# State products in a bank of their own, loads spread over chain steps, and a Horner form in the recurrent stage of a hybrid block

## The chip, the cores and the metric

The kernel runs on one core of a Trainium2 chip. The metric is the device time of the whole kernel in microseconds (us), the median of a few executions. TensorE is called PE below, its weight loads PEld, VectorE DVE, ScalarE ACT, GpSimd POOL, and SyncE SP. SP issues most of the DMAs.

## What is computed

The reference is one layer of a hybrid model on 1040 tokens (16 meta tokens and 1024 inputs) of width 1024: a norm, one input projection, an RWKV-7 recurrence over 16 heads of 64 dimensions, differential attention over 8 heads, a gated merge, and a mixture of 32 experts. The change touches the recurrence only:

```python
def step(state, inp):
    r_t, w_t, k_t, v_t, kk_t, a_t = inp
    sa = jnp.einsum('bhvk,bhk->bhv', state, -kk_t)
    state = (state * w_t[:, :, None, :]
             + sa[..., None] * (kk_t * a_t)[:, :, None, :]
             + v_t[..., None] * k_t[:, :, None, :])
    return state, jnp.einsum('bhvk,bhk->bhv', state, r_t)
```

## The kernel before

The kernel is a row of stages with a barrier between them: norm, two projections, attention, the recurrence (`rwkv`), merge, output and routing, experts, combine. The change lies in `rwkv`.

**Chunks.** The 1040 tokens are cut into 20 chunks of 52. Four heads are worked on at a time (index `d`, 0 to 3; `e` and `h` number the four heads, `h` being the upper or lower half of the partitions), so there are 80 chunks `ch`. A chunk has four kinds of work:

- `m` (`masked`): PE multiplies four pairs of chunk matrices for each head into PSUM (L1360), DVE masks the result into the tile `rw_M` (L1620). The PSUM bank is `ch % 2`, so bank 0 and bank 1 alternate.
- `tok`: PE turns three inputs by a product with the identity (L1435), ACT copies them to `rw_tok` (L1520).
- `solve`: a triangular inverse in steps 2, 6, 7, 8, 9, 10, 11, 12. Each step is a set of 52x52 products on PE and a copy by ACT (L1514) or an addition by DVE (L1634, L1644, L1631, L1649). Steps 10 to 12 make the second factor: step 10 gives Y and its transpose (copied by ACT to `rw_Y`), step 11 gives Y squared (copied by ACT), DVE makes G = I + Y from the copy in SBUF (L1631), and step 12 gives G + Y²G.
- `seq`: the chain over chunks, in steps q = 1 to 5. Step 1 multiplies the state by the keys (L1452, L1455), ACT negates it into `rw_R` (L1528). Steps 2 and 3 apply the two factors (L1459, L1464), each followed by an ACT copy (L1531, L1534). Step 4 makes the update of the state (L1471, L1473) in columns 384 to 511 of bank 6. DVE adds the old state (L1660, into `rw_St`) and multiplies by the chunk's decay `c.Pend` (L1662, into `rw_S`). Step 5 makes the chunk's output (L1479, L1481, L1484) in columns 256 to 383 of the same bank 6, and ACT copies it (L1541).

Before step 5 PE waits until DVE has finished with the bank:

```python
if t < NCH - 1:
    pe.wait_ge(seq_add, added(ch))
```

**Order.** `round_` writes the order out by hand. A round solves two chunks A and B at once, runs the chain for the two chunks of the round before, and makes the masked matrices of the two chunks ahead. There are 40 rounds and one more in which only the chain runs. Each engine walks the same list:

```python
return (step(2) + tokens(A) + piece() + step(6) + piece() + tokens(B) + step(7) + piece() + step(8) + piece() + piece()
        + step(9) + ahead(A + 2, 0) + piece() + step(10) + ahead(A + 2, 1) + piece() + step(11) + ahead(B + 2, 0) + piece()
        + step(12) + ahead(B + 2, 1) + piece() + piece())
```

The ten pieces of a round are q = 1 to 5 of one chunk and then of the next. A group norm over finished chunks (`gn`, seven times) is strewn over the pieces: DVE sums, ACT roots and evictions (L1549, L1559), POOL on large tiles (L1588 to L1603), PE transposes (L1497).

**Loads.** SP loads the five inputs of the next four heads in `load(d)`, ten DMAs of 520 KB back to back, once the chain has left the buffers. `load_rest(gi)` loads two more inputs for a group norm in four DMAs. `load_branch` brings in weights of the next stage. At the stage's start SP issues `load(1)`, two `load_branch`, `load_rest(0)` and `load_rest(1)`.

Of the kernel before, what the change touches and what calls it, by code (L numbers as in the profile page):

```python
# [12 lines left out]
ALU = mybir.AluOpType  # L13
# [7 lines left out]
TC = 52  # L21
NCH = T // TC
# [1186 lines left out]
def rwkv(nc, c):  # L1209

    with ExitStack() as st:
# [24 lines left out]
        Y1 = sb("rw_Y1", [128, 2, 2, 2, TC])  # L1236
        Y2 = sb("rw_Y2", [128, 2, 2, TC])
# [5 lines left out]
        St = sb("rw_St", [128, 2, RD])  # L1243
        bank = ps("rw_bank", [128, 8, 512])
        made, early_in = sem("rw_made"), sem("rw_early_in")
        emptied, tok_emptied = sem("rw_emptied"), sem("rw_tok_emptied")
# [3 lines left out]
        seq_dve, seq_act, seq_pe, seq_add = sem("rw_seq_dve"), sem("rw_seq_act"), sem("rw_seq_pe"), sem("rw_seq_add")  # L1250
# [7 lines left out]
        STEPS = {"pe": (2, 6, 7, 8, 9, 10, 11, 12), "dve": (2, 7, 8, 9, 11, 12),  # L1258
                 "act": (6, 7, 8, 10, 11), "pool": (6,)}
# [54 lines left out]
        @block.sync  # L1314
        def _(sp):
            def load(d):
                z = d % 2
                if d >= 2:
                    sp.wait_ge(seq_pe, seq_done(NCH * (d - 1) - 1, 5))
                for e in range(2):  # L1320
                    for dst, j in ((BK[z][:, e, 0], BHAT), (KR[z][:, e, 0], KAP), (KR[z][:, e, 1], RHAT), (BK[z][:, e, 1], KHAT),
                                   (V[z][:, e], VAL)):
                        sp.dma_start(dst, c.rwD[2 * d + e, j]).then_inc(x_in[z], 16)
# [24 lines left out]
        def _(pe):  # L1348
            def masked(ch, e):
                d, z, cols = place(ch)  # L1350
                if e == 0:
                    if ch == 0:
                        pe.wait_ge(emptied, 1 + OPEN)
                    if ch % NCH == 0:
                        pe.wait_ge(x_in[z], 160 * ((d + 1) // 2) + OPEN)
                    if ch > 1:
                        pe.wait_ge(m_read, ch - 1 + OPEN)
                for j in range(2):
                    for h in range(2):
                        last = mm(bank[here(h), ch % 2, (4 * e + 2 * j) * TC:(4 * e + 2 * j + 2) * TC].rearrange("p (a t) -> p a t", a=2),  # L1360
                                  BK[z][half(h), e, j, cols], KR[z][half(h), e, :, cols], start=True, stop=True)
                if e == 1:
                    last.then_inc(m_done, 1)

            def solve(ch, n):
# [4 lines left out]
                if n == 2:  # L1370
                    if ch == 0:
                        pe.wait_ge(emptied, 2 + OPEN)
# [66 lines left out]
            def seq(ch, q):  # L1439
# [25 lines left out]
                elif q == 4:  # L1465
# [3 lines left out]
                    for e in range(2):  # L1469
                        for h in range(2):  # L1470
                            mm(bank[half(h), 6, 384 + RD * e:384 + RD * e + RD], tok[here(h), s, 0, e, :], Uu[here(h), e, :], start=True, stop=False)  # L1471
                        for h in range(2):
                            last = mm(bank[half(h), 6, 384 + RD * e:384 + RD * e + RD], tok[here(h), s, 1, e, :], vv(e, h), start=False, stop=True)  # L1473
                else:
                    if t < NCH - 1:
                        pe.wait_ge(seq_add, added(ch))
# [27 lines left out]
        def _(act):  # L1504
            def solve(ch, n):
# [5 lines left out]
                        10: (Y1[0:PX, ln], four), 11: (Y2[0:PX, ln], two)}  # L1511
# [10 lines left out]
            def seq(ch, q):  # L1522
# [40 lines left out]
            nc.scalar.mul(bank[:, 6:8, :], c.eps[:].unsqueeze(2).to_broadcast([128, 2, 512]), 0.0).then_inc(tok_emptied, 1)  # L1563
# [4 lines left out]
        def _(pool):  # L1568
            over_heads = lambda j, n: gs[0:PX, j, 0:n].unsqueeze(2).to_broadcast([PX, n, RD])

            def solve(ch, n):
                ln = ch % 2
                eye = maskn[0:PX, 2].unsqueeze(1).to_broadcast([PX, 2, TC])
                if n == 6:
# [32 lines left out]
            walk({"solve": solve, "gn": norm})  # L1607

        @block.vector
        def _(dve):  # L1610
            tt, ts = nc.vector.tensor_tensor, nc.vector.tensor_scalar

            def masked(ch, e):
# [6 lines left out]
                tt(M4[0:PX, m], bank[0:PX, ch % 2, 0:8 * TC].rearrange("p (e k t) -> p e k t", e=2, k=4),  # L1620
                   mask4[0:PX].unsqueeze(1).to_broadcast([PX, 2, 4, TC]), ALU.mult).then_inc(m_read, 1)

            def solve(ch, n):
# [3 lines left out]
                if n in STEPS["dve"] and n != 11:  # L1627
                    dve.wait_ge(*at_pe(ch, n))
                if n == 11:
                    dve.wait_ge(*at_act(ch, 10))  # L1630
                    tt(G[0:PX, ln], Y1[0:PX, ln, 0], maskn[0:PX, 2].unsqueeze(1).to_broadcast([PX, 2, TC]),  # L1631
                       ALU.add).then_inc(sdve[ln], 1)
# [12 lines left out]
                elif n == 12:  # L1645
                    dve.wait_ge(*at_dve(ch, 11))
                    if ch >= TS4:
                        dve.wait_ge(seq_pe, seq_done(ch - TS4, 3))
                    tt(Gf[0:PX, ch % TS4], pairs(bq), G[0:PX, ln], ALU.add).then_inc(sdve[ln], 1)  # L1649

            def seq(ch, q):
                d, t = divmod(ch, NCH)
                if q == 4 and t < NCH - 1:
                    src = bank[:, 6, 384:512].rearrange("p (e d) -> p e d", e=2)
                    dve.wait_ge(seq_pe, seq_done(ch, 4))
                    if t == 0:
                        nc.vector.tensor_copy(St[:], src).then_inc(seq_add, 1)
                    else:
                        dve.wait_ge(seq_dve, added(ch - 1))
                        tt(St[:], src, S[:, t % 2], ALU.add).then_inc(seq_add, 1)  # L1660
                    dve.wait_ge(seq_add, added(ch))
                    tt(S[:, (t + 1) % 2], St[:], c.Pend[:, 2 * d:2 * d + 2, t:t + 1].to_broadcast([128, 2, RD]), ALU.mult).then_inc(seq_dve, 1)  # L1662
# [22 lines left out]
            nc.vector.memset(bank[:, 0:2, :], 0.0).then_inc(emptied, 1)  # L1685
            nc.vector.memset(bank[:, 2:6, :], 0.0).then_inc(emptied, 1)
# [1251 lines left out]
```

## Time and profile before

| | |
|---|---|
| time, median of 3 | 2832.94 us (2831.69 to 2835.86) |
| time of the profiled execution | 2827.87 us |
| its span, first to last instruction | 2826.1 us |
| the recurrent stage in it | from about 1212 us to about 1809 us of the span |
| mean granted TensorE clock, whole span | 0.966 |

The span is what the profile covers, and the device time of the same execution is 1.8 us longer. The stage begins where PE issues L1360 for the first time, and ends with the last copy of L1541 (it starts at 1807.82 us).

### The profile page before, as it was taken

The page shows a single profiled execution, that of the slowest core. Times are in us where ns is not written, and L with a number is a line of the kernel's source. Part 1 is how long each engine was busy: PE and PEld are TensorE (multiplying, and loading weights), DVE is VectorE, ACT ScalarE, POOL GpSimd, SP SyncE. Part 2 cuts the span into 40 slices and gives each one's busy share as a digit, 9 for nine tenths or more (in the row PEclk, how much of TensorE's full clock was granted, in tenths as well). Part 3 has the DMA queues.
Part 4 walks back from the last instruction along what each step waited for, and adds up shares of the span by engine and source line. Part 5 has one row for each costly group of instructions (what it writes and reads, how often), then busy time and mean ns, then how long its engine had stood idle before and what let it go on. Part 6 is the DMA issues. An engine that isn't in the chain of part 4 may idle for free. (4 is left out here: it accounts for less than half of the span.)

```text
span 2826.1 us, 64905 instructions
## 1 busy us (share of the span) xinstructions
PE 2584.2 (91%) x27593; PEld 2153.8 (76%) x27593; DVE 1571.1 (56%) x2294; ACT 1313.0 (46%) x2199; POOL 321.0 (11%) x367
## 2 busy tenths in 40 slices
PE   6999999999989999979888999799895999999992
PEld 5989886777766666778888888678784788888882
DVE  4566664442045555534344444553325888888885
ACT  5555542222134444324444444552222777777771
POOL 0121222331000000001212121200000000000002
PEclk9999999999999999989999999899996999999996
DMA  4443432212123224140202000144255999999976
GB/s 108 159 170 122 144 147 81 94 61 79 40 96 93 64 85 157 36 129 5 96 18 96 18 21 18 39 134 127 85 216 195 370 395 396 391 399 394 396 309 254
DMA packets 160693, 440.46 MB, mean 156 GB/s; under 512 B 14343, under 2 KB 94873, under 8 KB 148145
## 3 DMA queue, kind: packets, MB, share of 16 engines
q1 hardware_dynamic: 144461, 381.94, 37.6%
q10 hardware_dynamic: 9060, 29.56, 2.8%
q0 software_dynamic: 6912, 25.17, 2.3%
q8 instruction: 203, 3.33, 0.5%
q14 instruction: 57, 0.47, 0.1%
HBM read 344.22 MB, written 92.41 MB: 154 GB/s over the span
## 5 line engine op out<-in xcount | busy, mean ns | idle before, releaser
L2591 DVE TENSOR_TENSOR ex_wL<-wx,ex_wH 128x2048 fp32r<-128x2048 f32 x192 | 436.1, 2286 | 46.3 <-ACT ex_wH L2495 44.5
L2495 ACT CAST ex_wH<-wx 128x2048 fp32r<-128x2048 f32 x192 | 366.4, 1912 | 93.8 <-PE ex_bank L2391 70.6
L2389 PE MATMUL ex_bank<-ex_wH,ex_xTH 128*128 128x512 f32 x512 | 200.0, 391 | 2.4 <-DVE ex_xTL L2596 2.4
L2391 PE MATMUL ex_bank<-ex_wL,ex_xTH 128*128 128x512 f32 x512 | 199.8, 390 | 0.0
L2390 PE MATMUL ex_bank<-ex_wH,ex_xTL 128*128 128x512 f32 x512 | 199.7, 390 | 0.0
L709 PE MATMUL ph_acc<-ph_wH,uH 128*104 128x512 f32 x480 | 192.5, 401 | 6.5 <-DVE ph_wL L721 6.5
L709 PE MATMUL ph_acc<-ph_wH,uL 128*104 128x512 f32 x480 | 189.5, 395 | 0.0
L709 PE MATMUL ph_acc<-ph_wL,uH 128*104 128x512 f32 x480 | 189.5, 395 | 0.0
L413 PE MATMUL pf_acc<-uH,pf_wH 128*128 128x348 f32 x648 | 160.5, 356 | 6.3 <-DVE pf_wL L533 6.3
L413 PE MATMUL pf_acc<-uL,pf_wH 128*128 128x348 f32 x648 | 138.6, 322 | 0.0
L413 PE MATMUL pf_acc<-uH,pf_wL 128*128 128x348 f32 x648 | 138.3, 322 | 0.0
L413 PEld LDWEIGHTS pf_acc<-uH,pf_wH 128*128 128x128 f32 x648 | 110.7, 189 | 33.0 <-issue 11.6
L1644 DVE TENSOR_TENSOR rw_Q<-rw_bank,rw_Q 116x104 f32<-116x104 f32 x160 | 42.7, 267 | 158.8 <-PE rw_bank L1394 128.6
L1093 DVE TENSOR_REDUCE at_nmx<-at_bank 128x1 f32<-128x272 f32 (+7 forms) x128 | 93.0, 769 | 66.9 <-PE at_bank L1018 66.2
L1050 PEld LDWEIGHTS at_bank<-at_v,at_aT 128*128 128x128 f32 (+1 forms) x704 | 92.8, 189 | 45.9 <-ACT at_aT L1163 22.9
L2389 PE MATMUL ex_bank<-ex_wH,ex_hTH 128*128 128x512 f32 x256 | 103.9, 406 | 22.3 <-DVE ex_hTL L2601 22.3
L1050 PE MATMUL at_bank<-at_v,at_aT 128*128 128x128 f32 (+1 forms) x704 | 117.9, 296 | 4.1 <-ACT at_aT L1163 2.7
L1578 POOL TENSOR_TENSOR rw_Q<-rw_M,maskn 116x104 f32<-116x104 f32 x80 | 36.6, 459 | 745.1 <-DVE rw_M L1620 745.1
L1163 ACT COPY at_aT<-at_bank 128x512 f32<-128x512 f32 (+3 forms) x72 | 37.1, 515 | 175.3 <-PE at_bank L1040 175.3
L2389 PEld LDWEIGHTS ex_bank<-ex_wH,ex_xTH 128*128 128x128 f32 x512 | 96.5, 188 | 22.9 <-DVE ex_xTL L2596 2.8
L2391 PEld LDWEIGHTS ex_bank<-ex_wL,ex_xTH 128*128 128x128 f32 x512 | 96.4, 188 | 20.1
L2390 PEld LDWEIGHTS ex_bank<-ex_wH,ex_xTL 128*128 128x128 f32 x512 | 96.5, 188 | 20.0
(397 smaller groups left out, 6623.7 us busy)
## 6 DMA issues: line engine op xcount, KB each, us to landing
wx<-in_expert_w_gate SPq DMA_DIRECT2D x32, 2048.0 KB
wx<-in_expert_w_up SPq DMA_DIRECT2D x32, 2048.0 KB
wx<-in_expert_w_down SPq DMA_DIRECT2D x32, 2048.0 KB
s_y<-ex_y ACTq DMA_DIRECT2D x32, 512.0 KB, 10.1
fw<-in_w_in SPq DMA_DIRECT2D x27, 512.0 KB
hw<-in_w_in SPq DMA_DIRECT2D x6, 2048.0 KB, 10.1
s_qkT<-ph_stg ACTq DMA_DIRECT2D x4, 2080.0 KB, 6.9
mb_gt<-s_pT SPq DMA_DIRECT2D x16, 512.0 KB, 3.5
```

The source lines that it names most:

```text
L413: last = mm(acc[:, s, x, 0:CP], ww[:, s, k, :], uu[:, k, x * CP:(x + 1) * CP], start=(k == 0 and j == 0), stop=(k == KD - 1 and j == 2))
L709: last = nc.tensor.matmul(acc[:, slot, :], uu[:, k, t * TT:(t + 1) * TT], ww[:, b, k, :], start=(k == 0 and j == 0), stop=(k == KD - 1 and ...
L1050: last = nc.tensor.matmul(bank[:, PV:PV + 128], aT[0:rows_of(j), g % 2, 128 * x:128 * x + 128], v[0:rows_of(j), u // NS % 2, j, :], start= ...
L1093: nc.vector.tensor_reduce(nmx[:, u % 2, n:n + 1], bank[:, at:at + keys(u)], AX.X, ALU.max, negate=True).then_inc(maxed, 1)
L1163: nc.scalar.copy(aT[:, 0, 0:n], bank[:, TURN:TURN + n]).then_inc(moved_act, 1)
L1578: nc.gpsimd.tensor_tensor(Q[0:PX, ln, 0], M4[0:PX, ch % MS, :, 0, :], eye, ALU.add).then_inc(spool[ln], 1)
L1644: tt(dst, pairs(bq), Q[0:PX, ln, 1 - n % 2], ALU.add).then_inc(sdve[ln], 1)
L2389: nc.tensor.matmul(out, aH, bH, start=first, stop=False)
L2390: nc.tensor.matmul(out, aL, bH, start=False, stop=False)
L2391: return nc.tensor.matmul(out, aH, bL, start=False, stop=last)
L2495: nc.scalar.copy(wH[:, w, part], raw(j, s)[:, part]).then_inc(w_high, 1)
L2591: nc.vector.tensor_tensor(wL[:, w, part], raw(j, s)[:, part], wH[:, w, part], ALU.subtract).then_inc(w_low, 1)
```

## The change

Five things are changed in `rwkv`:

1. The state products of q = 4 go to bank 1, the masked matrices always to bank 0. PE no longer waits between q = 4 and q = 5; before each `m` it waits until DVE has read the chunk before.
2. The state update is split: ACT multiplies the old state by the decay after q = 1 (`SP`), and DVE does product times decay plus `SP` in one instruction for each `e`, in place of an addition and a multiplication.
3. The second factor is made by Horner's rule, I + Y(I + Y(I + Y)): PE makes the same number of products, ACT copies one 104-column tile at step 10 in place of a 208-column one and copies nothing at step 11, DVE adds the identity out of PSUM at steps 10, 11 and 12.
4. `load(d, n)` issues one DMA for each finished chain step (all five of its pieces), for ten chunks in a row. `load_rest(0)` comes first, the branch weights last. `load(1, 0)` waits for nothing.
5. The zeroing of PSUM at the start is shared out otherwise: DVE 416 and 1024 columns, ACT 624 in four pieces. POOL's copy of the diagonal block for step 7 moves forward in its own order, to the place of `m`.

```diff
             def load_rest(gi): ...
-            load(1)
+            load_rest(0)
+            for gi in range(1, 2 * ND):
+                if gi % 2 == 1 and gi // 2 + 1 < ND:
+                    for n in range(10):
+                        load(gi // 2 + 1, n)
+                load_rest(gi)
             for i in range(2):
                 load_branch(sp, c, c.w_branch_rwkv, c.bw[:, i], i, early_in)
-            load_rest(0)
-            load_rest(1)
-            for gi in range(2, 2 * ND):
-                if gi % 2 == 0 and gi // 2 + 1 < ND:
-                    load(gi // 2 + 1)
-                load_rest(gi)
+            def load(d, n):
+                z = d % 2
+                e, k = divmod(n, 5)
+                dst, j = (...)[k]
+                if d > 1 or n > 0:
+                    sp.wait_ge(seq_pe, seq_done(NCH * (d - 1) - 1 + n, 5))
+                sp.dma_start(dst, c.rwD[2 * d + e, j]).then_inc(x_in[z], 16)
 # PE, masked
-                    if ch > 1:
-                        pe.wait_ge(m_read, ch - 1 + OPEN)
+                    if ch > 0:
+                        pe.wait_ge(m_read, ch + OPEN)
-                        last = mm(bank[here(h), ch % 2, ...
+                        last = mm(bank[here(h), 0, ...
 # PE, solve
                 elif n == 10:
-                            mm(at(bx, 0, e, h), Nn[here(h), ln, 1, e, :], Qf[here(h), f, e, :], start=True, stop=True)
+                            mm(at(bx, 0, e, h), Qf[here(h), f, e, :], Nn[here(h), ln, 1, e, :], start=True, stop=True)
-                            last = mm(at(bx, 1, e, h), Qf[here(h), f, e, :], Nn[here(h), ln, 1, e, :], start=True, stop=True)
+                            last = mm(at(bq, 0, e, h), Nn[here(h), ln, 1, e, :], Qf[here(h), f, e, :], start=True, stop=True)
                 elif n == 11:
                     pe.wait_ge(*at_act(ch, 10))
+                    pe.wait_ge(*at_dve(ch, 10))
-                        last = mm(at(bx, 0, e, h), Y1[here(h), ln, 0, e, :], Y1[here(h), ln, 1, e, :], start=True, stop=True)
+                        last = mm(at(bx, 0, e, h), Y1[here(h), ln, e, :], G[here(h), ln, e, :], start=True, stop=True)
                 elif n == 12:
-                    pe.wait_ge(*at_act(ch, 11))
                     pe.wait_ge(*at_dve(ch, 11))
-                        last = mm(at(bq, 0, e, h), Y2[here(h), ln, e, :], G[here(h), ln, e, :], start=True, stop=True)
+                        last = mm(at(bq, 0, e, h), Y1[here(h), ln, e, :], G[here(h), ln, e, :], start=True, stop=True)
 # PE, seq 4 and 5
-                            mm(bank[half(h), 6, 384 + RD * e:384 + RD * e + RD], ...
+                            mm(bank[half(h), 1, RD * e:RD * e + RD], ...
                 else:
-                    if t < NCH - 1:
-                        pe.wait_ge(seq_add, added(ch))
 # ACT, seq 1
                     nc.scalar.mul(R[0:PX], src(0), -1.0).then_inc(seq_act, 1)
+                    if 0 < t < NCH - 1:
+                        act.wait_ge(seq_dve, added(ch - 1))
+                        for e in range(2):
+                            last = nc.scalar.mul(SP[:, e], S[:, t % 2, e], c.Pend[:, 2 * d + e, t:t + 1])
+                        last.then_inc(decayed, 1)
 # DVE, solve
-                if n == 11:
-                    dve.wait_ge(*at_act(ch, 10))
-                    tt(G[0:PX, ln], Y1[0:PX, ln, 0], maskn[...], ALU.add).then_inc(sdve[ln], 1)
+                if n >= 10:
+                    tt(Gf[0:PX, ch % TS4] if n == 12 else G[0:PX, ln], pairs(bx if n == 11 else bq), maskn[...],
+                       ALU.add).then_inc(sdve[ln], 1)
 # DVE, seq 4
-                        tt(St[:], src, S[:, t % 2], ALU.add).then_inc(seq_add, 1)
-                    dve.wait_ge(seq_add, added(ch))
-                    tt(S[:, (t + 1) % 2], St[:], c.Pend[...].to_broadcast([128, 2, RD]), ALU.mult).then_inc(seq_dve, 1)
+                        dve.wait_ge(decayed, (NCH - 2) * d + t + OPEN)
+                        for e in range(2):
+                            last = nc.vector.scalar_tensor_tensor(out=S[:, (t + 1) % 2, e], in0=src[:, e],
+                                                                  scalar=c.Pend[:, 2 * d + e, t:t + 1],
+                                                                  in1=SP[:, e], op0=ALU.mult, op1=ALU.add)
+                        last.then_inc(seq_dve, 1)
```

## Rows read from the trace of the kernel before

**Rows 1.** The page: busy time of PE, and the granted clock by slices.

```profile
PE 2584.2 (91%) x27593; PEld 2153.8 (76%) x27593; DVE 1571.1 (56%) x2294; ACT 1313.0 (46%) x2199; POOL 321.0 (11%) x367
...
PEclk9999999999999999989999999899996999999996
```

**Rows 2.** Busy time by stretches of the stage, the stretch in front.

```profile
core 0: us, PE busy (x) PEld busy (x) DVE busy (x) ACT busy (x) POOL busy (x), PEclk, DMA share, GB/s
1215.10:1252.30 37.20, 28.01 (x710) 26.96 (x708) 10.22 (x34) 9.55 (x31) 2.68 (x6) 0.77 0.73 199
1265.60:1374.60 109.00, 101.48 (x3461) 98.11 (x3457) 47.58 (x148) 49.23 (x168) 19.80 (x20) 1.00 0.02 4
1374.60:1444.00 69.40, 57.33 (x1729) 55.03 (x1726) 27.28 (x79) 25.40 (x87) 14.76 (x14) 0.90 0.35 111
...
1524.80:1589.30 64.50, 54.61 (x1729) 52.62 (x1725) 27.57 (x79) 25.36 (x87) 14.76 (x14) 0.95 0.38 119
...
1698.60:1728.90 30.30, 26.98 (x873) 26.14 (x871) 12.71 (x36) 12.31 (x43) 6.14 (x6) 0.94 0.15 35
```

**Rows 3.** Waits of PE's weight loads in the stage: us, times, longest.

```profile
PEld rw_bank L1479 <- DVE rw_St L1660: 35.0, 65, 0.6
...
PEld rw_bank L1400 <- issue: 7.7, 4, 3.6
...
PEld rw_bank L1479 <- DVE rw_St L1657: 2.2, 4, 0.6
```

**Rows 4.** Timeline around one step from q = 4 to q = 5.

```profile
1304.66 0.23 PEld L1473 LDWEIGHTS rw_bank<-rw_tok 52*64 52x64 f32 x4
...
1305.11 0.28 DVE L1660 TENSOR_TENSOR rw_St<-rw_bank,rw_S 128x128 f32<-128x128 f32 x1
...
1305.44 0.17 PEld L1479 LDWEIGHTS rw_bank<-rw_U,rw_M 52*52 52x52 f32 x4 [0.55 <-DVE rw_St L1660]
```

**Rows 5.** Timeline of the same round's second half, steps 10 to 12.

```profile
1301.51 0.28 ACT L1528 ACTIVATE rw_R<-rw_bank 116x128 f32<-116x128 f32 x1 [0.93 <-PE rw_bank L1455]
...
1301.90 0.72 ACT L1514 COPY rw_Y<-rw_bank 116x208 f32<-116x208 f32 x2
...
1302.60 0.48 PEld L1418 LDWEIGHTS rw_bank<-rw_Y 52*52 52x52 f32 x16
1302.64 0.59 DVE L1620 TENSOR_TENSOR rw_M<-rw_bank,mask 116x416 f32<-116x416 f32 x1 [1.68 <-PE rw_bank L1360]
...
1302.99 0.36 PEld L1360 LDWEIGHTS rw_bank<-kr,bk 64*52 64x52 f32 x8
```

**Rows 6.** Small DVE and ACT work of the stage by line: min/median/max ns.

```profile
L1660 DVE TENSOR_TENSOR rw_St<-rw_bank,rw_S x72: 280/291/293, 1251.3 to 1801.0; 128x128 f32<-128x128 f32 x72
L1631 DVE TENSOR_TENSOR rw_G<-rw_Y,maskn x80: 253/258/2222, 1226.1 to 1794.6; 116x104 f32<-116x104 f32 x80
L1649 DVE TENSOR_TENSOR rw_Gf<-rw_bank,rw_G x80: 253/267/268, 1226.9 to 1795.4; 116x104 f32<-116x104 f32 x80
L1514 ACT COPY rw_N<-rw_bank x80: 245/245/247, 1221.1 to 1788.8; 116x104 f32<-116x104 f32 x80
```

**Rows 7.** The same work as groups: busy us, mean ns, idle before.

```profile
L1549 ACT ACTIVATE rw_gs<-rw_gs,rw_geps 116x22 f32<-116x22 f32 (+1 forms) x7 | 2.2, 320 | 0.0
```

**Rows 8.** Timeline at 1424 us, where a POOL operation of the group norm runs.

```profile
1424.22 2.40 DVE L1631 TENSOR_TENSOR rw_G<-rw_Y,maskn 116x104 f32<-116x104 f32 x2
1424.24 2.25 POOL L1603 TENSOR_TENSOR mT<-rw_yw,rw_g 128x936 f32<-128x936 f32 x1
...
1426.77 0.40 PE L1423 MATMUL rw_bank<-rw_G,rw_Y 52*52 52x52 f32 x8 [1.71 <-DVE rw_G L1631]
```

**Rows 9.** PE's weight loads and clock while `load(2)` and `load_rest(2)` run.

```profile
1382.60 0.28 PEld L1400 LDWEIGHTS rw_bank<-rw_X 52*52 52x52 f32 x4 [3.58 <-issue]
...
1382.40:1389.20 6.80, 6.18 (x118) 6.03 (x120) 1.65 (x6) 1.03 (x4) 1.32 (x1) 0.50 1.01 411
```

More of the change, by code:

```diff
@@ L1315, in _ @@
         def _(sp):
-            def load(d):
+            def load(d, n):
                 z = d % 2
[L1318 to L1323, printed above, removed]
+                e, k = divmod(n, 5)
+                dst, j = ((BK[z][:, e, 0], BHAT), (KR[z][:, e, 0], KAP), (KR[z][:, e, 1], RHAT), (BK[z][:, e, 1], KHAT), (V[z][:, e], VAL))[k]
+                if d > 1 or n > 0:
+                    sp.wait_ge(seq_pe, seq_done(NCH * (d - 1) - 1 + n, 5))
+                sp.dma_start(dst, c.rwD[2 * d + e, j]).then_inc(x_in[z], 16)
             def load_rest(gi):
@@ L1355, in masked @@
                         pe.wait_ge(x_in[z], 160 * ((d + 1) // 2) + OPEN)
-                    if ch > 1:
-                        pe.wait_ge(m_read, ch - 1 + OPEN)
+                    if ch > 0:
+                        pe.wait_ge(m_read, ch + OPEN)
                 for j in range(2):
                     for h in range(2):
-                        last = mm(bank[here(h), ch % 2, (4 * e + 2 * j) * TC:(4 * e + 2 * j + 2) * TC].rearrange("p (a t) -> p a t", a=2),
+                        last = mm(bank[here(h), 0, (4 * e + 2 * j) * TC:(4 * e + 2 * j + 2) * TC].rearrange("p (a t) -> p a t", a=2),
                                   BK[z][half(h), e, j, cols], KR[z][half(h), e, :, cols], start=True, stop=True)
@@ L1470, in seq @@
                         for h in range(2):
-                            mm(bank[half(h), 6, 384 + RD * e:384 + RD * e + RD], tok[here(h), s, 0, e, :], Uu[here(h), e, :], start=True, stop=False)
+                            mm(bank[half(h), 1, RD * e:RD * e + RD], tok[here(h), s, 0, e, :], Uu[here(h), e, :], start=True, stop=False)
                         for h in range(2):
-                            last = mm(bank[half(h), 6, 384 + RD * e:384 + RD * e + RD], tok[here(h), s, 1, e, :], vv(e, h), start=False, stop=True)
+                            last = mm(bank[half(h), 1, RD * e:RD * e + RD], tok[here(h), s, 1, e, :], vv(e, h), start=False, stop=True)
                 else:
-                    if t < NCH - 1:
-                        pe.wait_ge(seq_add, added(ch))
                     for e in range(2):
@@ L1510, in solve @@
                 what = {6: (X2[0:PX, ln], four), 7: (X4[0:PX, ln], four), 8: (N8[0:PX, ln], two),
-                        10: (Y1[0:PX, ln], four), 11: (Y2[0:PX, ln], two)}
+                        10: (Y1[0:PX, ln], two)}
                 if n in what:
@@ L1561, in norm @@
                 ins.then_inc(gn["act"], 1)
-            nc.scalar.mul(bank[:, 6:8, :], c.eps[:].unsqueeze(2).to_broadcast([128, 2, 512]), 0.0).then_inc(tok_emptied, 1)
+            zero = lambda b, n: nc.scalar.mul(bank[:, b, 0:n], c.eps[:].to_broadcast([128, n]), 0.0)
+            for b, n in ((2, 4 * TC), (3, 2 * TC), (4, 4 * TC), (5, 2 * TC)):
+                last = zero(b, n)
+            last.then_inc(emptied_act, 1)
             act.wait_ge(made, 1 + OPEN)
@@ L1569, in _, with masked @@
             over_heads = lambda j, n: gs[0:PX, j, 0:n].unsqueeze(2).to_broadcast([PX, n, RD])
-            def solve(ch, n):
+            def masked(ch, e):
                 ln = ch % 2
                 eye = maskn[0:PX, 2].unsqueeze(1).to_broadcast([PX, 2, TC])
-                if n == 6:
+                if e == 1:
                     pool.wait_ge(m_read, ch + 1 + OPEN)
@@ L1605, in norm @@
                 ins.then_inc(gn["pool"], 1)
-            walk({"solve": solve, "gn": norm})
+            walk({"m": masked, "gn": norm})
         @block.vector
@@ L1619, in masked @@
                     dve.wait_ge(seq_pe, seq_done(ch - MS, 5))
-                tt(M4[0:PX, m], bank[0:PX, ch % 2, 0:8 * TC].rearrange("p (e k t) -> p e k t", e=2, k=4),
+                tt(M4[0:PX, m], bank[0:PX, 0, 0:8 * TC].rearrange("p (e k t) -> p e k t", e=2, k=4),
                    mask4[0:PX].unsqueeze(1).to_broadcast([PX, 2, 4, TC]), ALU.mult).then_inc(m_read, 1)
@@ L1653, in seq @@
                 if q == 4 and t < NCH - 1:
-                    src = bank[:, 6, 384:512].rearrange("p (e d) -> p e d", e=2)
+                    src = bank[:, 1, 0:2 * RD].rearrange("p (e d) -> p e d", e=2)
                     dve.wait_ge(seq_pe, seq_done(ch, 4))
                     if t == 0:
-                        nc.vector.tensor_copy(St[:], src).then_inc(seq_add, 1)
+                        tt(S[:, 1], src, c.Pend[:, 2 * d:2 * d + 2, 0:1].to_broadcast([128, 2, RD]), ALU.mult).then_inc(seq_dve, 1)
                     else:
-                        dve.wait_ge(seq_dve, added(ch - 1))
-                        tt(St[:], src, S[:, t % 2], ALU.add).then_inc(seq_add, 1)
-                    dve.wait_ge(seq_add, added(ch))
-                    tt(S[:, (t + 1) % 2], St[:], c.Pend[:, 2 * d:2 * d + 2, t:t + 1].to_broadcast([128, 2, RD]), ALU.mult).then_inc(seq_dve, 1)
+                        dve.wait_ge(decayed, (NCH - 2) * d + t + OPEN)
+                        for e in range(2):
+                            last = nc.vector.scalar_tensor_tensor(out=S[:, (t + 1) % 2, e], in0=src[:, e], scalar=c.Pend[:, 2 * d + e, t:t + 1],
+                                                                  in1=SP[:, e], op0=ALU.mult, op1=ALU.add)
+                        last.then_inc(seq_dve, 1)
             def norm(gi, name):
@@ L1683, in norm @@
                 ins.then_inc(gn["dve"], 1)
-            nc.vector.memset(bank[:, 0:2, :], 0.0).then_inc(emptied, 1)
-            nc.vector.memset(bank[:, 2:6, :], 0.0).then_inc(emptied, 1)
+            nc.vector.memset(bank[:, 0, 0:8 * TC], 0.0).then_inc(emptied, 1)
+            nc.vector.memset(bank[:, 6:8, :], 0.0).then_inc(tok_emptied, 1)
             nc.vector.memset(geps[:], GN_EPS).then_inc(made, 1)
```

28 lines of the change are left out of this document (12 added, 16 removed).

## The prediction

> **What bounds the kernel now.** I read the page first [rows 1]. PE is busy for 91% of the span, and the change touches one stage, 1212 to 1809 us. So the question is what PE loses in that stage. I then read the stage by stretches [rows 2], and chose the stretches so that one holds eight undisturbed rounds (1265.6 to 1374.6) and the others the three places where DMAs move many bytes. In the quiet stretch PE is busy 101.5 of 109.0 us, at the full clock (1.00, that is 2.4 GHz), and gets through 3461 matmuls, or 31.8 a microsecond. DVE is busy 44% and ACT 45% of it. PE is the bound, so a microsecond saved on PE's queue is worth a microsecond, and one on DVE or ACT is worth something only if PE waits for it.
>
> The view of waits then says for what PE waits [rows 3]. The largest entry is the wait between q = 4 and q = 5 for DVE's addition: 65 times and 35.0 us, and 4 times and 2.2 us for the first chunks. The next ones are "issue", stalls without a releaser, up to 3.6 us long.
>
> At the quiet rate the other stretches would take 710 / 31.8 = 22.4 us where they took 37.2; 1729 / 31.8 = 54.5 where they took 69.4; 54.5 against 64.5; and 27.5 against 30.3 [rows 2]. The excess is 14.8 + 14.9 + 10.0 + 2.8 = 42.5 us. This is an estimate, since a few matmul records may be missing.
>
> **The wait before q = 5 goes.** In the timeline the last weight load of q = 4 starts at about 1304.75 (the group starts at 1304.66, lasts 0.23, and one load takes about 0.14), and the first of q = 5 at 1305.44 [rows 4]. That is 0.69 us where neighbours follow each other in 0.04 or so, so 0.65 is lost, a little more than the idle time that the row prints. With 69 such waits [rows 3] and a mean loss that I take as 0.63: 69 x 0.63 = 43.5 us. Seven more have group-norm transposes between; I give them 0.2 each, together 1.4. Saved: 45 us. What is late next? q = 1 of the following chunk needs the new state. DVE's first instruction begins 0.36 us after that last load (1305.11), and two instructions of 64 columns follow. The nearest rows are 291 ns for 128 columns and 267 for 104 [rows 6], a slope of 1 ns a column, so 0.23 each; 0.29 bounds them from above, 0.20 from below. The state is there after 0.36 + 0.46 + 0.05 = 0.87 us. Between lie q = 5 (24 loads, 0.67 us) and the solve step and the matrices or turned inputs behind it (0.7 us or more), so nothing waits. If that cover were gone the cost would be at most 0.2 us a chunk.
>
> **The wait for bank 0 comes.** The second chunk's matrices (L1360 at 1302.99) now wait for DVE's read of the first's, which ends at 1302.64 + 0.59 = 1303.23 [rows 5]. A waiting PE starts 0.05 us after DVE ends (1305.39 to 1305.44 in [rows 4]). So PE stands from 1302.99 to 1303.28, 0.29 us a round: 39 x 0.29 = 11.5 us back. This recurs because the round's order is fixed. Bounds: 0, if PE comes there late for another reason, and 0.55 a round (21 us), if DVE's new step-10 additions push its read back by one of them, 0.27. The additions can start when step 10 is through, at about 1301.9 and 1302.3, and end by 1302.6, just before the read; I take 0.29. The other place where `m` follows `m` is half a round later, and DVE is long done. Queued behind the waiting PE are q = 3 and step 12, whose input from DVE (step 11) comes at about 1303.55, before PE is there.
>
> **The decay on ACT.** Two multiplications of 128x64 from SBUF for each of 72 chunks. No row shows this. The nearest are 245 ns for 104 columns from PSUM [rows 6] and 320 ns for 22 columns from SBUF, another function [rows 7]. I take 0.25 each and bound them by 0.20 and 0.35. In the second half of a round `rw_R` ends at 1301.79 [rows 5], the pair at 1302.3, the two step-10 copies, now 245 ns in place of 332, at 1302.8. Step 11 for the first chunk is due at 1302.60 and its copy ends at 1302.54: no wait. At the upper bound it waits 0.15 us, but PE would then stand less at bank 0, 0.4 us on, so nothing is added. In the first half the pair lies ahead of the step-6 copies, which have some 0.7 us to spare. ACT gets 36 us more of multiplications and loses 80 x 0.245 + 80 x 0.087 = 27 us of copies. In the seven group-norm evictions ACT is full for a while, for which I charge 2 us.
>
> **Horner.** PE makes the same products. DVE makes one more operation a chunk, 80 x 0.267 = 21 us of work, and the one at step 11 now reads PSUM (267 ns) in place of SBUF (258): hidden, as above, on an engine that is busy 44%. But it removes a collision. The additions of L1631 have a median of 258 ns and a longest of 2222 [rows 6], and at the long ones POOL works on a large tile and PE stands 1.7 us and loses 1.9 [rows 8]. DVE lines that read PSUM and one SBUF tile never exceed 293 ns in the stage. The new additions read PSUM. I count three stalls of 1.9 us (one each in the stretches at 1374, 1524 and 1698) and the reduced clock after two of them, 3.4 us at half rate, 1.7 each: 9 us saved; bounds 6 (the waits alone) and 11.
> The Trainium skill, SBUF — State Buffer, section Who interferes with whom, says the same of the mechanism: a VectorE instruction with two SBUF inputs contends with GpSimd reads, one with a single SBUF input does not. But the new state update has a scalar and a tile in SBUF, and if that counted as two inputs its price would be 7 group norms times some 1 us, 7 us at most; the sum would be 2 us saved here in place of 9.
>
> **The loads.** Of the 42.5 us excess, 9 are the collision's; 33 belong to the bulk loads. While they run at 411 GB/s PE stands 3.6 us on "issue" and then works at 0.50 of the clock, the 1.2 GHz level [rows 9], with 118 matmuls in 6.8 us where the quiet rate gives 216. I read the stalls as PE's instructions coming late through the same DMA engines. Spread out, one 520 KB load takes 520 / 411 = 1.3 us, and a delay of at most that should mostly vanish in what PE has buffered. What stays: at the start 1.7 MB in place of 8.6 (2 us), `load_rest` alone (three times about 1), the branch weights behind the last `load_rest` (3 us), and the 30 single loads at 0.1 each (3 us; bounds 0 and 0.7 each, the 1.3 us halved). Residue 11 us, saved 22; bounds 33 and 2.
> The Trainium skill, Runtime: NRT & Kernel Launch, section Instruction fetch mechanics, holds that crossing an instruction block is mostly hidden, since fetching keeps ahead of issue. By that rule the stalls are not a matter of the loads and spreading them gives nothing; the sum would be 39 us saved in place of 61. The rows with 3.6 us stalls beside full DMA engines speak against it.
>
> **The start.** PE waits for a memset of 1024 columns, 0.91 us, now 416 columns: 0.5 us saved. POOL's moved copy still waits for the same DVE read and has two rounds of slack: nothing.
>
> **Sum.** -45 + 11.5 + 2 - 9 - 22 - 0.5 = -63; I take 61, allowing 2 us for the event waits added on PE. Against the profiled execution, 2827.9 us, that gives 2767; it lies 5 us below the median of the runs, so the forecast for the median is 2832.9 - 61 = 2772 us.
>
> **The rivals.**
> - *The loads give nothing back* (each single load still delays PE's instructions by half its length, or the stalls have another cause): the 22 us are gone, 2794 us. For it: the stalls name no releaser. Against: they stand only in the stretches with bulk loads. 15%.
> - *New waits on ACT or DVE*: the bank wait at its upper bound (+10) and the decay showing on the chain by 0.15 us a chunk (+12), 2794 us. For it: second-half ACT has almost no slack. 14%.
> - *More than forecast*: no bank wait to speak of and hardly any residue, 2752 us. 8%.
> - *Slower*: ACT's decay decides. If one multiplication takes x, each round loses 2x - 0.86 in the second half (0.56 of slack at the copies, 0.3 absorbed at bank 0) and 2x - 0.74 in the first. To undo 61 us in 39 rounds takes 1.58 us a round, so x = 0.80 us. The rows give 0.25 to 0.32. 2%, and 1% for no change, x near 0.78. At x = 1 us the time would be 2833 - 61 + 39 x 2.4 = 2866.
> - *As forecast*: 60%, its own range 2762 to 2784.
>
> From these the range that leaves out no more than 2 in 10 is 2757 to 2796. Changes within 0.2%, 6 us, cannot be told from none. Faster 97%, same 1%, slower 2%.
>
> **What would show it.** PE's wait for `rw_St` is gone from the view of waits, and a new one of PE for `rw_M` stands there, about 39 times 0.2 to 0.3 us. Quiet rounds take 12.8 us where they took 109.0 / 8 = 13.6. The addition of step 11 never exceeds 0.3 us. "Issue" stalls of 3 us and the 0.50 clock after them are gone from the middle of the stage. The stage ends near 1748 us. The forecast is wrong if PE waits for ACT's `rw_Y` or `rw_R`, or if short "issue" stalls follow each single load.

## The result, and the profile after

The changed kernel takes 2801.66 us (median of 4, 2793.55 to 2807.62) against 2832.32 us for the kernel before. The ratio is 0.989, with a 95% interval of 0.9861 to 0.9919. The change is worth 31 us, half of the 61 forecast, and the time lies above the stated range. Its four times lie 14 us apart, which matters for the small differences below.

The profiled execution takes 2799.91 us. The page shows the stage's clock no longer dipping before its end, and PE as busy as it was:

```profile
PE 2574.8 (92%) x27593; PEld 2144.6 (77%) x27593; DVE 1558.3 (56%) x2370; ACT 1311.7 (47%) x2266; POOL 315.6 (11%) x367
...
PEclk9999999999999999999999999999996999999996
```

From the first product of the stage to the start of its last copy, 595.3 us have become 566.4, and of the stretches with the clock at half rate inside it (its first and last few us left out) 37.5 us have become 6.8. What follows the stage takes 1018 us before and 1020 after. The view of waits, PE's weight loads in the stage (us, times, longest), answers to [rows 3]:

```profile
PEld rw_bank L1357 <- DVE rw_M L1623: 8.7, 37, 1.1
...
PEld rw_bank L1391 <- issue: 6.4, 5, 1.9
PEld rw_bank L1461 <- issue: 5.4, 5, 2.4
PEld rw_bank L1397 <- issue: 4.1, 3, 1.7
PEld rw_bank L1432 <- issue: 3.8, 5, 2.3
PEld rw_bank L1373 <- issue: 3.8, 4, 2.5
PEld rw_bank L1389 <- issue: 3.3, 3, 1.4
PEld rw_bank L1449 <- issue: 3.1, 6, 1.0
```

The wait for `rw_St` is gone, and the wait for bank 0 is there 37 times at 0.24 us, as forecast. What is new is that "issue" stands at nearly every line of the stage: from 1216 to 1765 us these entries add up to 43.7 us in 55 waits. In the kernel before they were 36.3 us in 30 waits, the long ones beside the bulk loads and at the collision of [rows 8]. Three stretches without loads (busy time by stretches, as in [rows 2]):

```profile
core 0: us, PE busy (x) PEld busy (x) DVE busy (x) ACT busy (x) POOL busy (x), PEclk, DMA share, GB/s
1454.00:1494.00 40.00, 39.44 (x1318) 38.03 (x1314) 20.11 (x67) 20.28 (x73) 14.04 (x10) 1.00 0.02 5
1582.00:1635.00 53.00, 50.68 (x1706) 48.81 (x1702) 24.94 (x84) 25.21 (x94) 14.36 (x11) 1.00 0.02 5
1700.00:1757.00 57.00, 54.11 (x1819) 52.41 (x1820) 27.81 (x94) 24.96 (x94) 11.68 (x13) 1.00 0.02 5
```

That is 4843 matmuls in 150 us, 32.3 a microsecond. The quiet stretch before had 31.8 [rows 2]. My quiet round of 12.8 us in place of 13.6 would have been 31.8 x 13.6 / 12.8 = 33.8. So PE's quiet pace rose by 2% where 6% was forecast, with the full clock and almost idle DMA engines. But these stretches hold other parts of the rounds than the one before did, so the comparison is rough.

Like with like is the same round in both traces. I measured from the first product of step 2 in one round to that in the next, 39 distances, and call a round quiet when DMAs other than the instructions' moved less than 0.15 MB in it:

```
rounds                              before    after
16, quiet in both                   221.3     214.0 us
10, quiet before, with loads after  131.8     145.7
13, with loads before               214.8     182.5
```

A round that is quiet in both gained 0.46 us, where the forecast had 0.8. The 10 rounds into which loads were moved became 14 us longer, where 8 us less and a small residue were forecast: most of the shortfall of 30 us stands there.

**What the new stalls are.** The timeline of PE's weight loads across one of them, in the middle of the turned inputs of one chunk:

```profile
1606.77 0.47 PEld L1373 LDWEIGHTS rw_bank<-bk,kr 64*52 64x52 f32 x16
1607.16 0.23 PEld L1432 LDWEIGHTS rw_bank<-ident,bk 64*52 64x52 f32 x5
1608.27 0.34 PEld L1432 LDWEIGHTS rw_bank<-ident,bk 64*52 64x52 f32 x10 [0.88 <-issue]
```

No wait stands in the program between two products of this group. The trace's DMA records have a queue of their own for instructions (137 transfers of 16 KB in this stage, in which PE's records are 17223 weight loads, as many matmuls and 569 waits, so some 256 instructions a transfer). I set their landings beside PE's stalls within one line, a stall being a distance of 0.35 us or more from the start of one weight load or matmul to the start of the next. For three stalls of the stretch above, in us:

```
stall begins  length  block transfer starts  lands     PE resumes  after landing
1584.53       0.58    1582.93                1583.88   1585.11     1.23
1607.32       0.95    1605.96                1606.92   1608.27     1.36
1611.57       0.73    1609.80                1610.98   1612.30     1.33
```

All 39 such stalls (38.4 us) end 1.20 to 1.61 us after the landing of an instruction block, median 1.36. No two blocks start less than 3.28 us apart, and the median is 3.92. In the kernel before there were 17 stalls of this length (25.9 us). Three of them are the collision of [rows 8] and one more is a short one at the stage's start; the other 13 (19.9 us) end at the same distance from a landing. Blocks came at a median of 3.93 us.

Where they stand matters. In the changed kernel 32 of the 39 (34.1 us) lie in the 22 rounds in which other DMAs move 0.15 MB or more. The 17 quiet rounds have 7 (4.3 us), 1.9% of their time against 0.8% in the 26 quiet rounds of the kernel before. So PE waits for late blocks mainly in the rounds with loads; in the quiet ones this explains only a part of what is missing, and the rest is not attributed.

**The other steps in the profile.** Durations by line (min/median/max ns), for ACT's decay, DVE's state update and the additions of the second factor:

```profile
L1527 ACT ACTIVATE rw_SP<-rw_S,Pend x144: 334/338/341, 1233.6 to 1770.7; 128x64 f32<-128x64 f32 x144
L1660 DVE SCALAR_TENSOR_TENSOR rw_S<-rw_bank,Pend,rw_SP x144: 273/275/286, 1237.4 to 1773.3; 128x64 f32<-128x64 f32 x144
...
L1635 DVE TENSOR_TENSOR rw_G<-rw_bank,maskn x160: 254/266/268, 1223.2 to 1767.2; 116x104 f32<-116x104 f32 x160
```

The 2222 ns of [rows 6] are gone, and the state update never exceeds 286 ns. ACT's multiplication is near my upper bound of 0.35. The bank wait looks like this:

```profile
1591.43 0.59 DVE L1623 TENSOR_TENSOR rw_M<-rw_bank,mask 116x416 f32<-116x416 f32 x1 [0.16 <-PE rw_bank L1357]
...
1592.07 0.35 PEld L1357 LDWEIGHTS rw_bank<-kr,bk 64*52 64x52 f32 x8 [0.27 <-DVE rw_M L1623]
```

PE resumes 0.05 us after DVE ends at 1592.02, as at 1305.44 in [rows 4].

### The profile page after: what moved, and what is told of

Read it like the earlier page. It is cut to its first block and busy times, and to the rows that moved or that the text cites. A ratio compares the mean times of both kernels' runs of the same rounds, so it can differ in the third digit from the quotient of the medians.

```text
span 2798.2 us, 65045 instructions
## 1 busy us (share of the span) xinstructions
PE 2574.8 (92%) x27593; PEld 2144.6 (77%) x27593; DVE 1558.3 (56%) x2370; ACT 1311.7 (47%) x2266; POOL 315.6 (11%) x367
```

## The experiments

Theory A: PE's instruction supply is the bound of the quiet rounds. Its rivals: the spreading of the loads was worth its price and something else failed; PE's array work is the bound; the stalls are hidden waits (theory C). All runs have 4 to 12 times of their own, and the runs of a group share those of the kernel before (2831.75, 2831.83 and 2831.89 us). Differences against the changed kernel lean on its four times, and I estimate from their scatter and that of the runs that some 8 us can't be told from none. Of each kernel there is one trace, and the sums of its stalls vary too (e2).

**e1, the old order of loads in the changed kernel.**

```diff
-            load_rest(0)
-            for gi in range(1, 2 * ND): ... for n in range(10): load(gi // 2 + 1, n)
+            load(1); branch weights; load_rest(0); load_rest(1)
+            for gi in range(2, 2 * ND): ... load(gi // 2 + 1) ... load_rest(gi)
```

> The changed kernel with the old order of loads: ten 520 KB loads back to back for each group of four heads, branch weights early. Theory A (instruction supply): PE's instructions come in blocks through the same DMA engines, one block per 3.5 to 3.9 us, and the change left no slack, so each of the 30 single loads costs about 1.2 us, which is as much as the bundles cost before; the time stays within 8 us of the changed kernel's 2802. Rival, my forecast's price: spreading saved 22 us and something else fell short; then this kernel takes about 2823 us. Theory C (the issue stalls are hidden waits for other engines and have nothing to do with DMAs): no change, 2802, and the stalls stay where they are.

Measured: 2816.72 us (ratio to before 0.995, 0.9937 to 0.9963). Spreading is worth 15 us here: more than the 8 us that theory A allowed and less than the 22 of my forecast. In this run's trace the half-rate stretches are back (34.1 us). It also shows the change without single loads: the 26 rounds that are quiet here and in the kernel before take 344.9 us in place of 353.1, 0.32 a round where 0.8 was forecast.

**e2, the changed kernel with 10 of its 30 loads.**

```diff
-                if gi % 2 == 1 and gi // 2 + 1 < ND:
+                if gi == 1:
```

> The changed kernel without the 20 loads for the third and fourth group of heads; these groups compute on the inputs and decays of the first two. Theory A: 20 loads at 1.2 us, 24 us less than the changed kernel, about 2778 us, and quiet rounds still show short issue stalls of 0.4 to 1 us at the pace of the instruction blocks. The forecast's price of 0.1 us a load: 2 us less. Theory C: no change.

Measured: 2796.33 us (0.9871, 0.9855 to 0.9887), 5 us less than the changed kernel, a difference within the scatter. Taken as it is, 20 loads cost 5.3 us, 0.27 each; that is far from 1.2. The traces show more: the 12 rounds in which the bytes of the 20 loads moved are 14.6 us shorter without them (0.7 a load), with 7.8 us of stalls in place of 19.9. But the other 27 rounds, with the same instructions and the same bytes, are 9 us longer in this trace, with 26.9 us of stalls in place of 18.6. So stalls thicken where loads run and come without them too, their sum can differ by 8 us between two traces of the same work, and a single load costs between 0.3 and 0.7 us.

**e3, products of half the width.**

```diff
-   mm(bank[here(h), 0, (4 * e + 2 * j) * TC:(4 * e + 2 * j + 2) * TC]..., BK[z][half(h), e, j, cols], KR[z][half(h), e, :, cols], ...)
+   mm(bank[here(h), 0, (4 * e + 2 * j) * TC:(4 * e + 2 * j + 1) * TC], BK[z][half(h), e, j, cols], KR[z][half(h), e, 0, cols], ...)
```

> The changed kernel with the masked products at half width: 52 columns in place of 104, with the same number of instructions. The query half is left out, so the outputs miss that term. A 104-column product takes PE 0.040 us from load to load, a 52-column one 0.0245, so 32 x 0.0155 = 0.5 us a round. If PE's own work is the bound: 39 x 0.5 = 20 us less, about 2782. Theory A: the time is set by how many instructions PE needs, and these stay; at most 6 us less, 2796 or more.

Measured: 2806.67 us (0.9912, 0.9898 to 0.9926), no gain at all. Its quiet stretches:

```profile
1454.00:1494.00 40.00, 37.37 (x1262) 35.25 (x1258) 18.23 (x65) 19.33 (x70) 15.09 (x11) 1.00 0.02 5
1582.00:1635.00 53.00, 50.25 (x1729) 48.24 (x1727) 25.16 (x86) 25.42 (x95) 15.63 (x13) 0.98 0.02 4
1700.00:1757.00 57.00, 53.13 (x1838) 50.54 (x1836) 27.45 (x94) 25.42 (x95) 11.63 (x13) 1.00 0.02 5
```

4829 matmuls in 150 us, the pace of the changed kernel (4843), with less array work in each. The stalls of the kind above grew from 39 to 59 (55.9 us), 58 of them within 1.65 us of a landing, and in the quiet rounds from 4.3 us to 13.8. Of the 20 us that the array should save, 17.5 come back in the trace as waiting for instructions. This rules out array work alone as the bound.

**e4, part 1 alone in the kernel before.**

```diff
-   bank[half(h), 6, 384 + RD * e:384 + RD * e + RD]
+   bank[half(h), 1, RD * e:RD * e + RD]
-                    if t < NCH - 1:
-                        pe.wait_ge(seq_add, added(ch))
-   bank[here(h), ch % 2, ...]   # wait m_read for ch - 1
+   bank[here(h), 0, ...]        # wait m_read for ch
```

> The kernel before with part 1 alone: state products in bank 1, masked matrices in bank 0, no wait before q = 5. DVE still adds and multiplies. If the removed wait is worth what it measured (45 us) less the wait for bank 0 (12 us): 33 us less than before, about 2800. Theory A: PE runs into the pace of its instruction blocks in every quiet round and gets back only 0.3 us of the 0.85 in each: about 12 us less than before, 2820.

Measured: 2818.36 us (0.9947, 0.9934 to 0.996), 13.4 us less than before, as theory A had it, and 20 short of the 33 of my sum. In its trace the stalls that end 1.1 to 1.7 us after a landing number 35 (34.1 us), against 13 (19.9 us) in the kernel before: taking the wait away brought them. But part of the 20 us is something else. This kernel still multiplies by the decay on DVE, and PE waits for it at q = 1, which it never did before:

```profile
PE rw_bank L1452 <- DVE rw_S L1660: 3.7, 6, 1.2
```

The trace is of the slowest of the six executions (2832.80 us), so its sums are rather too high.

**e5, part 4 alone in the kernel before** (the diff of e1 the other way round).

> The kernel before with part 4 alone: loads one per chain step, branch weights last. In the changed kernel this part is worth 15 us (it against the run with bulk loads). If PE's instruction supply has slack in the kernel before (0.3 to 0.4 us a block, since PE still waits before q = 5), single loads hide better here than in the changed kernel: 15 to 22 us less than before, 2810 to 2817. If the parts just add up: 15 less.

Measured: 2820.83 us (0.9964, 0.9949 to 0.9979), 11 us less than before. My idea that single loads would hide better where PE has slack is not borne out: 11 here, 15 there, which the scatter doesn't tell apart.

**e6, half of the identity products as transposes.**

```diff
-   last = mm(bank[here(h), 7, ...], src, c.ident[half(h), half(h)], start=True, stop=True)
+   last = (tr(bank[here(h), 7, ...], src, c.ident[half(h), half(h)]) if h == 0 else mm(...))
```

> The changed kernel with half of its identity products (those of the lower half of the partitions, six a chunk) written as transposes, which the trace shows as one weight load and one matmul where the product takes two of each. 24 instructions fewer a round, of about 900. Theory A (instruction supply): 24 / 256 of a block of 3.5 us, 0.33 us a round, 13 us less than the changed kernel, about 2789. Rival (PE's own work is the bound): the array time saved is 12 loads at 0.0245, 0.3 us a round, nearly the same; so this run alone can't tell the two apart, the half-width products and the added waits do. If hidden waits for other engines are the bound (theory C): no change.

Measured: 2938.54 us (1.0366, 1.0342 to 1.0391), 137 us slower: a miss of all theories. The timeline of PE's weight loads has one chunk's first 12 of them:

```profile
1306.36 1.56 PEld L1432 LDWEIGHTS rw_bank<-ident,bk 64*52 64x52 f32 x12
```

The timeline of the kernel before has 16 such loads in 0.52 us:

```profile
1306.50 0.52 PEld L1435 LDWEIGHTS rw_bank<-ident,bk 64*52 64x52 f32 x16
```

So it is 0.13 us from load to load in place of 0.02 to 0.03; I read this as a transpose not overlapping with the ordinary product of the other partition half next to it. The stage of this trace also has 133 us at half rate in place of 14, so the 137 us are not only the transposes' own. This run says nothing on the supply.

**e7, 32 more waits a round that are already met.**

```diff
                 at = lambda b, k, e, h: ...
+                for _ in range(2 if ch > 1 else 0):
+                    pe.wait_ge(emptied, 1 + OPEN)
```

> The changed kernel with two more waits on PE ahead of every solve step, on a semaphore that has long been there: 32 instructions more a round that do nothing for the result. Theory A: 32 / 256 of a block of 3.5 us, 0.44 us a round, 17 us more than the changed kernel, about 2819. Rival (the array's work is the bound and the sequencer runs ahead of it): no change within 5 us. If each costs the 0.05 us that the trace shows for such an instruction, and nothing hides it: 1.6 us a round, 62 us more.

Measured: 2825.19 us (0.9969, 0.9958 to 0.998), 23.5 us more than the changed kernel. PE's wait records in the stage rose by only 624 (569 to 1193), half of the waits that the program has more. So a recorded wait costs 0.038 us, more than its share of a block (3.5 us by 256 instructions, 0.014) and less than the 0.05 us of its record. An array that works while the sequencer runs ahead is ruled out as the bound. The stalls rose to 62 (57.7 us), each within 1.65 us of a landing; the traced execution is the slowest of the eight.

**e8, part 3 alone in the kernel before** (steps 10 to 12 as in the change's diff).

> The kernel before with part 3 alone: the Horner form. My forecast's price: the three long stalls of PE for the addition out of SBUF (1.9 us each) and the low clock after two of them are gone, 9 us less, 2823. Rival: PE gets nothing from it because it runs into its instruction blocks or waits for the longer DVE chain: within 3 us of the kernel before. In the trace the longest addition of the second factor is 0.3 us either way.

Measured: 2827.66 us (0.9984, 0.9973 to 0.9996), 4.2 us less than before (1 to 8 by the interval), half of the 9 forecast, and less than the 6.5 us that PE spent waiting for L1631 in the kernel before:

```profile
PE rw_bank L1423 <- DVE rw_G L1631: 6.5, 6, 1.7
```

**e9, two products of step 7 merged.** They share the stationary matrix, so one call with 104 moving columns replaces two. To fit this, ACT copies the result of step 7 in two instructions, one of them after DVE's addition, and step 8 makes its products in another order.

```diff
-   mm(at(bx, 0, e, h), X2[here(h), ln, 1, e, :], X2[here(h), ln, 0, e, :], ...)
-   last = mm(at(bq, 0, e, h), X2[here(h), ln, 1, e, :], Q[here(h), ln, 0, e, :], ...)
+   mm(bank[here(h), bx, 0:4 * TC]...[:, :, e, :], W[here(h), ln, 2, e, :], W[here(h), ln, 0:2, e, :], ...)
```

> The changed kernel with two products of step 7 that share a stationary matrix made as one with 104 moving columns: 320 calls fewer, 1280 of PE's about 35,000 instructions in the stage, or 5 instruction blocks. ACT and DVE then share a bank, so ACT's copy of half of the result waits for DVE; I charge up to 0.1 us a round, 4 us. Theory A (instruction supply): 5 x 3.5 = 17 us less, minus up to 4: 2785 to 2789. Rival (the array's work): 16 times 2 x 0.0245 - 0.040 = 0.009, 0.15 us a round, 6 us less, and the 4 us lost: 2800.

Measured: 2798.28 us (0.989, 0.9873 to 0.9906), 3.4 us less than the changed kernel, within the scatter. The 5 blocks are gone (132 in place of 137) and the stalls fell from 38.4 to 29.7 us, but the saving is spent elsewhere: the mean distance of the weight loads that follow each other without a stall rose from 28.0 to 29.2 ns. By an estimate 0.7 of these 1.2 ns come from the new mix alone, 640 loads at 0.040 us in place of 1280 at 0.0245; the rest is not attributed. Counting blocks alone is too simple. This was theory A's miss.

**e10, waits that another wait implies are dropped.**

```diff
-                    if ch > 0:
+                    if ch % 2:
                         pe.wait_ge(m_read, ch + OPEN)
-                    pe.wait_ge(m_read, ch + 1 + OPEN)           # step 6
-                    pe.wait_ge(tok_read, ch + 1 + OPEN)         # q = 1, kept for ch == 0
-                    pe.wait_ge(*at_dve(ch, 12))                 # q = 3, kept for the last two
```

> The changed kernel without PE waits that another wait implies (before every second masked product, in step 6, in q = 1 for the turned inputs, in q = 3). The run with more waits put the price of a recorded wait at about 0.038 us. Up to 7 a round go, of which some are no instruction of their own. Theory A: 4 to 7 a round, 39 x 0.038 x 4 to 7 = 6 to 10 us less than the changed kernel, 2792 to 2796. Rival: waits that are already met cost nothing; no change.

Measured: 2792.14 us (0.9863, 0.9845 to 0.988), 9.5 us less than the changed kernel with 164 fewer wait records, 0.06 us each. The stalls fell to 24.2 us. This difference alone is barely clear of the scatter.

**e11, both of these.**

> The changed kernel with the merged products of step 7 and without the implied waits. Theory A: the savings add up, 13 to 17 and 6 to 10 us: 2775 to 2783. Rival: 2800.

Measured: 2785.18 us (0.9835, 0.982 to 0.9851), 16.5 us less than the changed kernel and 46.7 less than before. It beats both and lies 2 us above what was expected. Against e9 the dropped waits are worth 13.1 us here, which bears e10 out.

**e12, part 2 undone in the changed kernel.**

```diff
-                            last = nc.vector.scalar_tensor_tensor(out=S[...], in0=src[:, e], scalar=c.Pend[...], in1=SP[:, e], ...)
+                        tt(SP[:], src, S[:, t % 2], ALU.add).then_inc(decayed, 1)
+                    dve.wait_ge(decayed, added(ch))
+                    tt(S[:, (t + 1) % 2], SP[:], c.Pend[...].to_broadcast([128, 2, RD]), ALU.mult).then_inc(seq_dve, 1)
```

> The changed kernel with part 2 undone: DVE adds the old state and multiplies by the decay, in two instructions of 128 columns, and ACT has no multiplications by the decay. If part 2 is free, as forecast: within 3 us of the changed kernel, 2799 to 2805. Rival: ACT's two multiplications (0.34 us each in the changed trace) delay its copies, and the time falls by 5 us or more without them.

Measured: 2811.69 us (0.9937, 0.9919 to 0.9954), 10 us more than the changed kernel, a little more than the scatter. Part 2 is not neutral but worth some 10 us. The line of the multiplication, and PE's waits for it:

```profile
L1656 DVE TENSOR_TENSOR rw_S<-rw_SP,Pend x76: 291/399/2068, 1233.8 to 1780.8; 128x128 f32<-128x128 f32 x76
```

```profile
PE rw_bank L1449 <- DVE rw_S L1656: 5.3, 8, 1.9
```

A multiplication with both inputs in SBUF takes up to 2.07 us beside a POOL operation, and now that PE doesn't wait before q = 5 it reaches q = 1 too early. In the kernel before the same multiplication made PE wait nowhere, though it too was stretched:

```profile
L1662 DVE TENSOR_TENSOR rw_S<-rw_St,Pend x76: 291/398/1391, 1242.8 to 1801.3; 128x128 f32<-128x128 f32 x76
```

Of the 10 us these waits explain 5.3; the rest is not attributed.

## Why the prediction was half right

- **The wait before q = 5 and the wait for bank 0: the failed step.** Both waits moved exactly as forecast (the first to nothing, the second to 37 times 0.24 us idle, against 39 times 0.29). Their worth did not: part 1 alone gives 13.4 us (e4), not 33, and with the 10 us of part 2, which takes DVE's multiplication out of PE's way (e12), some 23 if the two add. What failed is the sentence "a microsecond saved on PE's queue is worth a microsecond". PE's waits before q = 5 also gave its instruction blocks time to arrive. With them gone PE stands until 1.2 to 1.6 us after a block's landing, 39 times in the stage. Evidence: the landings, the rounds that are quiet in both kernels (0.46 us gained where 0.8 was due) and in e1 (0.32), e4 (13 stalls after landings became 35), e3 (less array work, no gain), e7 and e10 with e11 (more and fewer wait instructions, 23.5 us slower and 9.5 to 13 us faster). In the quiet rounds of the changed kernel itself the long stalls are 4.3 us only, so there the missing 0.3 us a round is in part unexplained.
- **The loads.** The mechanism was right: the 3.6 us stalls and the half clock leave with the bundles, all but 6.8 us at half rate, and return with them (e1). The term of 22 us measured 11 (e5) and 15 (e1). The single loads cost 0.3 to 0.7 us each (e2), above the 0.1 that I took and up to my bound of 0.7. "Short issue stalls follow each single load" was one of my signs that the forecast is wrong, and it came in large part: 32 of the 39 stalls stand in the rounds with loads. The Trainium skill, Runtime: NRT & Kernel Launch, section Instruction fetch mechanics, says that a block of 256 instructions is refilled while the current one runs and that this is mostly hidden. The 16 KB transfers agree with the block; that it stays hidden does not hold here, with 39 stalls of 38.4 us in one stage.
- **Horner and the collision.** Right in kind: the addition no longer exceeds 268 ns. The term of 9 us measured 4.2 (e8).
- **The decay on ACT.** Cost of one: 0.34 us, near the upper bound; PE waits for none of ACT's copies in any new place. But I gave the part a price of 2 us. It is worth some 10 us (e12), at least in part because part 1 uncovers DVE's two-input multiplication. I had named the cover ("if that cover were gone") with 0.2 us a chunk, from undisturbed rows, and missed the disturbed ones. The Trainium skill, SBUF — State Buffer, section Who interferes with whom, says that a VectorE instruction with two SBUF inputs contends with a GpSimd instruction that reads SBUF, and that one with at most one SBUF input does not. The trace agrees: up to 2068 ns for the first kind (e12). The new update reads PSUM, a tile and a scalar, and never exceeds 286 ns, so the scalar did not count as a second input.
- **The parts together.** Alone in the kernel before, parts 1, 3 and 4 give 13.4 + 4.2 + 11.0 = 28.6 us. Together without part 2 (and with the small part 5) they give 20 (2831.9 - 2811.7), and part 2 adds 10. The 8 us between the two sums are about what the scatter of such a sum allows.
- **The rivals.** "New waits on ACT or DVE" and "the loads give nothing back" both gave 2794, and the time came 8 us above them. The first did not happen. The second did in its mechanism (single loads delay PE's instructions) but not in its size, since the loads gave 11 to 15 us back. The cause that I had not listed is that the removed wait was the blocks' slack.

What stays open: how much of the loss is the late landing of blocks and how much PE's own issue time for each wait instruction (0.04 to 0.06 us in e7 and e10). The runs change both at once. Open too is what an undisturbed round lacks beyond its long stalls, and why e9 gained only 3.4 us.

## What to carry to other kernels

- A stream of short matmuls can be held up by the supply and issue of instructions while PE shows 92% busy. Set PE's stalls beside the landings on the instruction queue: if they end a fixed time after a landing, look for fewer instructions and fewer waits rather than shorter products (e3, e11).
- Compare the same rounds before and after, not averages over stretches: here that showed which rounds gained and which lost.
- Before you price the removal of a wait, ask what it was hiding: here instruction blocks, and a DVE instruction that POOL sometimes stretches to 2 us.
- A wait that another wait implies isn't free: dropping 164 of them gave 9.5 us (e10), and 13 in the kernel with merged products (e11).

## What the runs showed of the hardware

- PE resumed 1.2 to 1.6 us after the landing of an instruction block of 16 KB in all 39 stalls of the changed kernel; the transfer took 1.0 us at the median; and no two blocks started less than 3.23 us apart in this stage in any of the 14 traces.
- A recorded wait on PE that is already met cost 0.038 us (e7), and the removal of one saved 0.06 us (e10; 9.5 us by 164).
- Transposes alternating with ordinary products on the two halves of the partitions ran at 0.13 us from load to load in place of 0.02 to 0.03; the kernel became 137 us slower, with 133 us of the stage at half rate in place of 14 (e6).
- A 128x64 multiplication on ACT out of SBUF took 338 ns, where a 116x104 copy out of PSUM took 245 [rows 6].
